# Four quadrants turned by a transfer instead of by TensorE, in a fused convolution and MLP layer

## The reference

```python
h = rmsnorm(x, mix_norm)
b_gate, c_gate, v = split(h @ conv_w_in, 3)       # 2048 x 6144
u = c_gate * v
y = causal depthwise convolution of u, width 3
x = x + (b_gate * y) @ conv_w_out                 # 2048 x 2048
h = rmsnorm(x, mlp_norm)
a = relu(h @ mlp_w1)                              # 2048 x 8192
out = x + (a * a) @ mlp_w2                        # 8192 x 2048
```

## Time and profile before

| | us |
|---|---|
| median of 3 runs | 1896.21 (1895.91 to 1896.45) |
| the profiled execution | 1895.67 |
| its span | 1893.9 |
| TensorE busy | 1885.1 (100%) |
| VectorE busy | 1677.6 (89%) |
| ScalarE busy | 1060.2 (56%) |
| GpSimd busy | 150.9 (8%) |

### The profile page before, as it was taken

The page is one execution under the profiler, slowest core; times in us unless marked ns, Lnnn a source line. Parts: engine busy times, 40 slices in busy tenths (PEclk is TensorE's granted clock), DMA queues, the critical chain, the costliest instruction groups (busy, mean ns, idle before and its releaser), DMA issues.

```text
span 1893.9 us, 22247 instructions
## 1 busy us (share of the span) xinstructions
PE 1885.1 (100%) x8476; PEld 1561.7 (82%) x8476; DVE 1677.6 (89%) x1500; ACT 1060.2 (56%) x1134; POOL 150.9 (8%) x242
## 2 busy tenths in 40 slices
PE   9999999999999999999999999999999999999999
PEld 8888888888888888888888888888888888888887
DVE  6688999899999898989989899898998889788878
ACT  6474664755548577586675866755444333433332
POOL 0100011000011111120111201100000000000000
PEclk9999999999999999999999999999999999999999
DMA  9795768859677966887968879699988878877783
GB/s 370 262 289 146 268 215 317 258 142 357 198 204 287 351 239 209 321 295 238 362 221 316 294 239 363 223 398 401 359 342 342 337 289 315 353 308 283 293 327 119
DMA packets 153946, 542.05 MB, mean 286 GB/s; under 512 B 44528, under 2 KB 48624, under 8 KB 128880
## 3 DMA queue, kind: packets, MB, share of 16 engines
q1 hardware_dynamic: 119712, 416.85, 57.9%
q0 software_dynamic: 33984, 123.75, 21.4%
q10 hardware_dynamic: 144, 0.04, 0.0%
HBM read 438.35 MB, written 94.37 MB: 281 GB/s over the span
## 4 chain that ended last, share of the span: by engine, by line
PE 93%; DVE 4%; issue 1%; DMA 1%; ACT 0%; SPq 0%; DVEq 0%; ACTq 0%
PE pair L1324 87%; PE pair L1337 5%; PE pair L1355 2%; DVE ring L1022 1%; DMA raw<-in_turns 1%; DVE raw L1016 1%; DVE sum_l_mix L1053 0%; DVE sum L1053 0%; DVE sum L1051 0%; DVE sum_first_mix L1065 0%; DVE quads L920 0%; DVE stage L1003 0%; ACT ring L663 0%; DVE sum_l_mix L1065 0%; DVE sum_first_mix L1053 0%
## 5 line engine op out<-in xcount | busy, mean ns | idle before, releaser
L1324 PE MATMUL pair<-ring,act 128*128 128x512 f32 x7728 | 1765.4, 390 | 2.5 <-DVE ring L1022 1.4
L1324 PEld LDWEIGHTS pair<-ring,act 128*128 128x128 f32 x7728 | 1447.0, 188 | 304.3 <-issue 5.3
L663 ACT ACTIVATE ring<-raw 128x1024 fp32r<-128x1024 f32 x659 | 695.5, 1058 | 758.6 <-PE pair L1324 480.1
L1022 DVE TENSOR_TENSOR ring<-raw,ring 128x1024 fp32r<-128x1024 f32 x659 | 791.4, 1221 | 153.5 <-ACT ring L663 151.7
L1016 DVE TENSOR_TENSOR raw<-raw 128x1024 f32<-128x1024 f32 x312 | 367.8, 1220 | 9.4 <-DMA raw<-in_turns 1.2
L530 POOL DMA_DIRECT2D spill<-stage x136 | 78.6, 617 | 486.4 <-ACT stage L802 370.9
L543 POOL DMA_DIRECT2D raw<-in_turns x56 | 50.4, 1053 | 696.2 <-DVE raw L1016 696.2
L1003 DVE TENSOR_TENSOR stage<-quads,stage 128x1024 fp32r<-128x1024 f32 x68 | 83.1, 1222 | 24.7 <-ACT stage L802 23.1
L1337 PE MATMUL pair<-ring,act 128*128 128x512 f32 x384 | 87.6, 390 | 1.2 <-DVE ring L933 1.2
L1337 PEld LDWEIGHTS pair<-ring,act 128*128 128x128 f32 x384 | 71.9, 188 | 16.5 <-issue 1.6
L802 ACT ACTIVATE stage<-quads 128x1024 fp32r<-128x1024 f32 x68 | 71.5, 1051 | 15.9 <-DVE quads L920 6.9
(11 more groups left out here) (109 smaller groups left out, 539.9 us busy)
## 6 DMA issues: line engine op xcount, KB each, us to landing
raw<-in_turns SPq DMA_DIRECT2D x191, 1024.0 KB, 7.4
act<-spill SPq DMA_DIRECT2D x290, 512.0 KB, 6.8
spill<-stage POOLq DMA_DIRECT2D x136, 512.0 KB, 9.3
act<-act_kept SPq DMA_DIRECT2D x74, 512.0 KB, 8.6
raw<-in_turns POOLq DMA_DIRECT2D x56, 512.0 KB, 8.6
act_kept<-act POOLq DMA_DIRECT2D x28, 512.0 KB, 9.8
x_tok<-in_x SPq DMA_DIRECT2D x4, 1024.0 KB, 14.1
x<-mixed SPq DMA_DIRECT2D x8, 512.0 KB, 15.5
```

Source lines behind the costliest of these rows:

```text
L663: nc.scalar.activation(ring[g % RING][:, 0], raw[:, raw_of(v, s), 2 * (s % 2):2 * (s % 2) + 2, :], ACT.Copy).then_inc(hi_ready, 1)
L1022: nc.vector.tensor_tensor(ring[g % RING][:, 1], raw[:, raw_of(v, s), 2 * (s % 2):2 * (s % 2) + 2, :], ring[g % RING][:, 0].bitcast(F32), A ...
L1324: mm = nc.tensor.matmul(bank, stationary, moving, start=(opens and k == 0 and n == 0), stop=(closes and k == NT - 1 and n == 2))
```

## The change

The last quadrant (`m` = 3) of the two GATE and the two MIXED pairs, in turns 6, 12, 14 and 16, is turned by a transposing transfer. ScalarE writes its planes in slot 5 and joins the turned halves in slot 8, for a GATE pair into the new tile `joined` (in the place of planes that are then free, and of the padded `u`, whose first two columns VectorE sets to zero again), for a MIXED pair into the quadrant itself, where four scaled copies follow. VectorE's product for a GATE pair's last quadrant reads `joined` and stands at slot 9, and not at slot 7. One pair of ScalarE's squares (`square_mixed`) goes from slot 8 to 9, and the direct splits and forms of turns 12 and 16 stand at other slots. `by_transfer` also takes one off what TensorE waits for before it writes the bank `pairs[1]` with L12.

```diff
 def by_transfer(q):
-    return 2 if KINDS[q] == GATED else int(KINDS[q] == UP and q < NQP - 1)
+    return 2 if KINDS[q] == GATED else int(q < NQP - 1)
...
+JOINED = [sum(KINDS[p] != GATED for p in range(q)) for q in range(NQP + 1)]
...
-    DIRECT_SPLIT.update({(_v, 8): (_d, L11), (_v, 9): (_d, S1), (_v, 11): (_d, S2), (_v, 12): (_d, L12),
+    DIRECT_SPLIT.update({(_v, 7): (_d, L11), (_v, 10): (_d, S1), (_v, 12): (_d, S2), (_v, 13): (_d, L12),
...
+        joined = at("joined", PLANES_AT[2], [P, NT, HALF])
...
                 if KINDS[q] == GATED:
                     act.wait_ge(u_formed, FORMED_U[q] + (2, 4, 2, 4)[m])
+                elif m < 4 - by_transfer(q):
+                    act.wait_ge(quad_turned, TURNED[q] + m + 1)
                 else:
-                    act.wait_ge(quad_turned, TURNED[q] + m + 1)
+                    act.wait_ge(planes_out, 2 * TRANSFERS[q + 1])
...
+                elif KINDS[q] == MIXED:
+                    act.wait_ge(added, pair_added(q) + FINISHED[m])
                 else:
                     act.wait_ge(rectified, RECTIFIED[q] + 2 * m + 2)
+                    act.wait_ge(y_step, 2 * FORMED_U[q])
...
-            def square_planes(q):
-
-                act.wait_ge(planes_in[2], 16 * (q - UP0 + 1))
+            def join_planes(q, o):
+
+                act.wait_ge(planes_in[2], 16 * (JOINED[q] + 1))
                 quads_free(act, q)
-                o = quad["L21"]
                 words = o.bitcast(U16).rearrange("p a (t z) -> p z (a t)", z=2)
                 for z in range(2):
                     nc.scalar.activation(words[:, z], turned_words(q, 3, z).rearrange("p a t -> p (a t)"),
                                          ACT.Copy).then_inc(merged, 1)
...
+            def take_mixed_planes(q):
+                join_planes(q, quad["L21"])
+                act.wait_ge(merged, 2 * (JOINED[q] + 1))
+                for i in range(NT):
+                    tile = MLP + NT * (q - MIX0) + i
+                    o = quad["L21"][:, i, :]
+                    ins = nc.scalar.activation(o, o, ACT.Copy, scale=cols[:, tile:tile + 1])
+                ins.then_inc(quad_ready, 1)
...
-                        if kind == UP and by_transfer(q - 1) and s == 5:
+                        if kind != GATED and by_transfer(q - 1) and s == 5:
                             put_planes(q - 1, 3)
+                        if kind == GATE and s == 8:
+                            join_planes(q - 1, joined[:])
+                        if kind == MIXED and s == 8:
+                            take_mixed_planes(q - 1)
...
-                        if kind == MIXED and s in (3, 5, 6, 7):
-                            take_mixed(q - 1, {3: 0, 5: 1, 6: 2, 7: 3}[s])
-                        if kind == MIXED and s in (4, 8, 10, 11):
-                            square_mixed(q - 1, *{4: (1, 0), 8: (2, 1), 10: (0, 2), 11: (3, 3)}[s])
+                        if kind == MIXED and s in (3, 5, 6):
+                            take_mixed(q - 1, {3: 0, 5: 1, 6: 2}[s])
+                        if kind == MIXED and s in (4, 9, 10, 11):
+                            square_mixed(q - 1, *{4: (1, 0), 9: (2, 1), 10: (0, 2), 11: (3, 3)}[s])
...
+            def gate_joined(q):
+                dve.wait_ge(merged, 2 * (JOINED[q] + 1))
+                dve.wait_ge(y_step, 2 * FORMED_U[q])
+                o = quad["L21"]
+                nc.vector.tensor_tensor(o, joined[:], o, ALU.mult).then_inc(quad_ready, 1)
+                if q == Z0:
+                    dve.wait_ge(quad_ready, TURNS[q + 1])
+                    nc.vector.memset(u_pad[:, :, 0:CW - 1], 0.0).then_inc(pad_ready, 1)
...
-                    gated_late = v < V_DOWN and v % 2 == 0 and KINDS[q - 1] == GATE and s in (5, 6, 7)
-                    if gated_late:
-                        gate(q - 1, {5: 1, 6: 2, 7: 3}[s])
+                    gated_late = v < V_DOWN and v % 2 == 0 and KINDS[q - 1] == GATE and s in (5, 6, 9)
+                    if gated_late and s == 9:
+                        gate_joined(q - 1)
+                    elif gated_late:
+                        gate(q - 1, {5: 1, 6: 2}[s])
```

More of the change, by code:

```diff
@@ L110 @@
 for _d, _v in ((2, V_OUT), (3, V_UP)):
-    DIRECT_SPLIT.update({(_v, 8): (_d, L11), (_v, 9): (_d, S1), (_v, 11): (_d, S2), (_v, 12): (_d, L12),
-                         (_v, 13): (_d, S3), (_v + 1, 1): (_d, S4), (_v + 1, 3): (_d, L22)})
-    DIRECT_FORM.update({(_v, 8): (_d, (0,)), (_v, 10): (_d, (1,)), (_v, 11): (_d, (2,)), (_v, 12): (_d, (3,))})
+    DIRECT_SPLIT.update({(_v, 7): (_d, L11), (_v, 10): (_d, S1), (_v, 12): (_d, S2), (_v, 13): (_d, L12),
+                         (_v + 1, 0): (_d, S3), (_v + 1, 1): (_d, S4), (_v + 1, 3): (_d, L22)})
+    DIRECT_FORM.update({(_v, 9): (_d, (0,)), (_v, 11): (_d, (1,)), (_v, 12): (_d, (2,)), (_v, 13): (_d, (3,))})
 DIRECT_ORDER = [(0, L12), (0, L22), (0, S3), (1, L11), (1, L21), (0, S1), (0, S2), (0, S4), (1, L12), (1, L22), (1, S3),
@@ L745, in square_planes @@
                                          ACT.Copy).then_inc(merged, 1)
-                act.wait_ge(merged, 2 * (q - UP0 + 1))
-                o = o.rearrange("p a t -> p (a t)")
+            def square_planes(q):
+                join_planes(q, quad["L21"])
+                act.wait_ge(merged, 2 * (JOINED[q] + 1))
+                o = quad["L21"].rearrange("p a t -> p (a t)")
                 nc.scalar.activation(o, o, ACT.Square).then_inc(quad_ready, 1)
+            def take_mixed_planes(q):
+                join_planes(q, quad["L21"])
+                act.wait_ge(merged, 2 * (JOINED[q] + 1))
+                for i in range(NT):
[3 more added lines that the diff above has]
+                ins.then_inc(quad_ready, 1)
             def by_channels():
@@ L755, in take_u @@
                 act.wait_ge(y_step, 2 * FORMED_U[q])
-                act.wait_ge(pad_ready, 1)
+                act.wait_ge(pad_ready, 1 + int(q > Z0))
                 first = 2 * (CW - 1 + HALF * half)
```

## The result

The changed kernel takes 1905.66 us (median of six runs, 1905.13 to 1906.29) against 1896.06 for the kernel before: ratio 1.0052, 95% interval 1.0039 to 1.0065. It is slower by 9.6 us, as forecast in sign; the predicted 1902.6 is 3 us short, and the range up to 1905.5 just misses it.

The account below looks back on a forecast made before the run. TensorE bounds the kernel, but in turns 14 to 17 a ScalarE and VectorE chain runs beside it with under a microsecond of cover. 1895.67 + 9.2 - 2.0 - 0.5 = 1902.4, predicted 1902.6 us, range 1896.5 to 1905.5.

Parts of the forecast that it names:

- The mixer turns: Turns 14 to 17: ScalarE's additions lengthen its chain with VectorE; TensorE 9.2 us late, both additions in full.
- ScalarE's 4.6 us: Added in each of the four turns: 1.99 us for two plane copies and 2.58 for two joins.
- VectorE's wait of 0.94 us at 640.03: VectorE's gap in the mixer turns, for a transfer its own earlier add releases; claimed to move along, giving no catch-up.
- rival 3: Transfer lands late in turns 14 and 16, ScalarE stands before the join: 4 us more, 1906.6 us; chance 0.08.
- The wait that was taken at nothing: ScalarE's wait for the transfer before the join: landing 3.7 to 6.2 us after issue, covered by some 8 us of steps.
- a sign of being wrong: ScalarE standing before a join for the transfer, listed among what would show the prediction wrong.
- Turn 12: Gate pair: VectorE's waits of 1.27 and 0.63 us and TensorE's stop at 519.31 go; gain 2.0 us.
- Turn 6: Gate pair: TensorE gains 0.9 us, kept only if turn 7's weights land earlier; gain taken as 0.5 us.
- The sentence before it: Turn 6: first weight load issued some 1.2 us earlier; if the whole queue moves up, all 0.9 us is gained.
- The sum: Whole kernel: 1895.67 + 9.2 - 2.0 - 0.5 = 1902.4 us; on the median 1902.9, predicted 1902.6.
- Rival 1: Whole kernel: TensorE's gain arrives and ScalarE's copies hide in its waits; 1891.6 us; chance 0.10.
- Rival 2: Mixer turns: only the plane copies count, joins hide, 1.1 us each turn; about 1897 us; chance 0.17.

Follow-up runs that it names:

- the run alone: Kernel before with only the named turns' pairs by transfer: mixer turns 14 and 16 1907.33 us, turn 12 1893.83 us, turn 6 1897.65 us.
- The useless copies: Kernel before, all quadrants on TensorE, plus unread ScalarE copies in slots 5 and 8 of turns 14 and 16, no transfer or join: 1902.51 us.
- the run with the plane copies behind: Against the run with the mixer pairs alone, plane copies moved behind the second quadrant's copies in slot 5 of turns 14 and 16: 1905.96 us.
- the run with the mixer pairs alone: Kernel before with only the last quadrants of turns 14 and 16 by transfer: 1907.33 us, ratio 1.0058.
- the run with the moved squares: Against the run with the mixer pairs alone, six ScalarE squares moved from turn 14 to 15 and two from 16 to 17: 1903.71 us.

## Why the prediction was right and where it failed

**The mixer turns: right, a little small.** The term was 4.6 + 4.6 = 9.2; the traces show 4.14 + 5.72 = 9.9, the run alone 10.9. The mechanism was as put: ScalarE's 4.6 us lengthen the chain of ScalarE and VectorE, from split to split by 3.9 and 6.1 us. The useless copies (+6.1 for 8.0 us of them) and the run with the plane copies behind (a change within the intervals) show it. That the trace comes so close to 9.2 is in part luck, for two things were missed that nearly cancel. In turns 14 and 15 VectorE's wait of 0.94 us at 640.03, which was to move along, shrank to 0.23: 0.7 us of cover, and 3.9 where 4.6 stood. In turns 16 and 17 it grew by 6.1 where 4.6 stood. There ScalarE stood 0.96 us before the joins, as its timeline and the chain of the changed kernel (start us, us, what) show:

```profile
670.50 2.59 ACT L750 ACTIVATE quads<-planes_t 128x1024 uint16<-128x1024 uint16 x2 [0.96 <-DMA planes_t<-planes]
```

```profile
659.54 2.00 ACT planes L738 x2
...
661.55 8.93 DMA planes_t<-planes
...
670.50 2.60 ACT quads L750 x2
```

The transfer took 8.93 us, where the longest before was 6.2: a little of rival 3, which was costed from 8 us on. The wait that was taken at nothing, and named as a sign of being wrong, is not of one execution only: in turn 16 ScalarE stands 0.96 to 1.60 us there in all four profiles with these joins in slot 8, and not at all in turn 14. How much of the 0.7 us (by the traces) to 1.7 us (by the run alone) over the forecast it makes was not separated.

**Turn 12: right.** -2.0 forecast, -2.14 in the traces of turns 12 and 13, -2.6 by the run alone. VectorE's wait for the fourth quadrant and TensorE's stop in slot 12 are gone, and ScalarE's three waits for TensorE, 1.66, 1.66 and 1.60 us, have become one of 0.57 and one of 0.16: there its added steps did fall into waits.

**Turn 6: the step that failed.** "Between 0 and 0.9 I take 0.5" as a gain; the run alone measured +1.2 us (from 0.2 under before to 3.2 over), the changed kernel 3.2 us more in turns 6 to 8. The sentence before it asked only whether R21 would land earlier, and looked at VectorE and at SyncE's queue for it: that half held (with the spill kept in place, R11 is issued 1.4 us earlier in turn 6, though the three loads behind it only 0.1; R21 lands in 15.0 us, and the gain is 2.9, more than the 0.9 that I allowed at most). What was missed is the third list. ScalarE's join in slot 8 stands ahead of its split of the L12 quadrant, GpSimd's spill waits for that split, and spills and weights share the DMA engines: with the join ahead R21 landed after 19.2 us, with the join behind the split after 15.0. I worked out ScalarE's added 4.6 us for turns 12, 14 and 16 and, in turn 6, not at all; "VectorE is at work without such waits there" made me think only of VectorE. So the lower bound of zero had no reason behind it.

**The sum.** 6.7 us over its execution was forecast, 9.6 measured. By the single runs, 2.8 of the 2.9 us are 1.7 for turn 6 (-0.5 against +1.2) and 1.7 for the mixer turns (9.2 against 10.9), less 0.6 for turn 12 (-2.0 against -2.6); each is known to about 2 us.

**The rivals.** Rival 1 is out: the copies don't hide in the mixer turns. The Trainium skill ("Perfetto Trace Analysis", section "Identifying the Most-Contended Engine") uses the occupancy percentage to judge an engine like ScalarE. Taken over the whole span, 57%, it would have had ScalarE carry the copies; taken over the stretch that mattered, 32.24 of 32.70 us, it would not, and the times side with the stretch. Rival 2 is out: by it the mixer turns cost 2.2 us, and they cost 9.9. Rival 3 is seen in part, in turn 16.

## What to carry to other kernels

Give every added instruction a line in each list that it enters, and follow who waits behind it, as far as the transfers that are issued from there: two copies, 2.6 us together, ahead of a spill moved the landing of a weight load by 4 us, and exchanging the two steps was worth 4 us of the kernel. Read an engine's room in the slots where the work is to stand; room in the next turn did not help. Where a load's wait differs between executions by a microsecond, as here in turn 7, a single profile of the kernel before is not the baseline.

## What was not expected of the hardware

In the run with the mixer pairs alone TensorE's granted clock fell after a stop of 2.07 us in turn 16. Windows of TensorE (us, busy us, PEclk, DMA share, GB/s):

```profile
686.00:688.00 2.00, 0.04 (x1) 1.00 0.54 225
688.00:689.00 1.00, 0.89 (x3) 0.66 0.00 0
689.00:689.50 0.50, 0.50 (x3) 0.50 0.00 0
...
690.00:691.00 1.00, 1.00 (x3) 0.50 0.50 188
691.00:692.00 1.00, 1.00 (x4) 0.64 0.98 418
692.00:693.00 1.00, 1.00 (x6) 1.00 0.86 360
```

For some 3 us it stands at 0.50, the level of 1.2 GHz, and matmuls run at half rate (3 in a microsecond, where there are 6 at 1.00), which costs some 1.7 us; the same happened in turn 14 after its stop of 2.02 us, and in the run with the moved squares in turn 16 after one of 2.11. The profiled execution of the changed kernel, with stops of 1.93 and 2.10 us at the same places, kept 1.00. Why one and not the other stays open. It doesn't explain what this run took over the 9.9 us of the changed kernel: the two of its executions with a mean clock of 1.000 took 1907.59 and 1908.77 us, the profiled one, with 0.998, 1905.92.
